# The blocked inverse in the second mixer: its dense chunks gathered in front of it and at its end

## The chip, the cores and the metric

One core of one Trainium2 chip. The metric is device microseconds (us) of one execution of the whole kernel, the median of the runs shown. Lower is better.

## The reference, cut to what matters

The kernel computes two transformer blocks on x of 256 tokens by 1024 features, all in float32. The change lies in the second block's mixer. Its left half (8 heads of 64) is a generalised delta rule, computed in 4 chunks of 64 tokens; its right half (another 8 heads) is softmax attention with forgetting:

```python
p = h @ w_in[l]
p_rwkv = token_shift(p[..., :SHIFT_COLS], shift_mu[l])
p_fox = p[..., SHIFT_COLS:SHIFT_COLS + FOX_COLS]
gates = jax.nn.sigmoid(p[..., SHIFT_COLS + FOX_COLS:])
...
sa = jnp.einsum('bhvk,bhk->bhv', state, a_t)
state = (state * w_t[:, :, None, :]
         + sa[..., :, None] * b_t[:, :, None, :]
         + v_t[..., :, None] * k_t[:, :, None, :])
y_t = jnp.einsum('bhvk,bhk->bhv', state, r_t)
```

Inside a chunk the kernel does not step token by token. It writes the 64 dependent steps as a unit triangular system and inverts that matrix for each of 32 head-chunks: blocks of 2 are inverted first, and 5 levels then double the block size (2 to 64) by X <- X + X N X, where N is the part of the matrix below the blocks (m_b under a mask of `levels`).

## The kernel before, in words

**Weights.** The weights come as chunks of 1 MB (128 x 2048 float32), numbered in the order of their use, in a ring of 3 slots. SyncE loads chunk n once the low part of chunk n-3 is made. ScalarE copies it to `w_hi` (L1489, it waits for the slot's chunk n-3 to be used), VectorE takes the rest, `w_lo = w_raw - w_hi` (L1813), and TensorE runs three matmuls for each product of a step: high by high, high by low, low by high (L2253 to L2255, called `three`). A chunk by `columns` or by tokens is 8 steps (`NT`) of 6 matmuls; these are called dense here. `columns(n, steps=(a, b))` does steps a to b-1 of chunk n, so a chunk can be spread over other work. A dense chunk goes to one of the PSUM banks 0 to 2 (n % 3), and its reader's count `bank.._read` lets the chunk 3 later start.

**The inverse** (`pe_mixer`, L594 to L655). The 16 unit columns of both head halves are treated in two sets, f = 0 and f = 1, of 8 units by 2 heads. For level n (1 to `LEVELS` = 5) and set f:

- GpSimd makes `half_n`, N under the mask of level n (L1457), a level ahead; it signals `off_ready`.
- `first_product(n, f)` on TensorE: N X into PSUM bank 4 (L599). It waits for `off_ready`, for the copy out of bank 4 before, and for `x_added` of level n-1 of its own set. 32 instructions in the trace.
- ScalarE copies bank 4 to `half_1` (L871), signal `p1_copied`.
- `second_product(n, f)` on TensorE (L599 also): X-transposed by that copy into bank 6 or 5, and the transposed result into bank 7 or 3; 64 instructions, and 32 at level 5, where the first of the two is left out. It waits for `p1_copied` and for the bank's reader, `xt_added`.
- `grow(n, f)` on VectorE adds bank 6 or 5 to `x_inv` (L1098, signal `x_added`) and bank 7 or 3 to `xt_inv` (L1101, signal `xt_added`).

Each engine's order is written out by hand. TensorE's order before: `first_product(n,0)`, `second_product(n-1,1)`, `second_product(n,0)`, `first_product(n,1)`, then a piece of a dense chunk. The chunks cut up for this are B_FOX+3 (`fk`, the attention's keys), B_FOX+4 and B_FOX+5 (its values, by tokens) and step 0 of B_GA, the first chunk of gates. ScalarE's queue holds, between the copies of `half_1`, the high parts of chunks B_FOX+5 (level 1), B_FOX+6 = B_GA (level 2) and B_FOX+7 (level 4), and `v_tokens(0)` ahead of level 4, which takes the values of B_FOX+4 out of PSUM (L862). VectorE's holds the low parts of the same chunks and, at level 1, `out_bank(B_FOX+3)` (L1850).

**Around it.** In front stand the chunk scores (L573), transposes (L487, L589) and one step of B_FOX+3. Behind it stands a loop over 4 chunks (L657 to L703, L668 in the trace) in which small products, copies by ScalarE (L878, L880, L882) and sums by VectorE (L1117, L1119) follow one another; step 1 of B_GA lies in its last turn, step 2 behind it (L705), and then the head sums of y (L708) and the rest of the gates.

Of the kernel before, what the change touches and what calls it, by code (L numbers as in the profile page):

```python
# [11 lines left out]
ACT = mybir.ActivationFunctionType  # L12
# [6 lines left out]
NT = D // P  # L19
# [69 lines left out]
def block_pair(nc, inp, out, scratch, shifted):  # L89

    ctx = ExitStack()
    with ctx:
        S = Signals(nc, ctx)
# [5 lines left out]
        bank = [side_banks[b // 2][:, b % 2, :] for b in range(4)]  # L99
# [376 lines left out]
        def pe_mixer(told, pe, state, by_columns, by_tokens, by_rows, rows_to_tokens, turn_late_half, spread):  # L476
            def columns(n, fresh=None, tokens=False, midway=None, steps=(0, NT)):
                if steps[0] == 0:
                    pe.wait_ge(S[f"bank{bank_of[n]}_read"], reads[n] - 1)
                if tokens:  # L480
                    by_tokens(n, n % RING, bank_of[n], steps=steps)
                else:
                    by_columns(n, n % RING, bank_of[n], fresh=fresh, midway=midway, steps=steps)
# [107 lines left out]
                                   start=True, stop=True)  # L591
            mm.then_inc(S["units_turned"], told.one("units_turned"))

            columns(B_FOX + 3, steps=(1, 4))  # L594

            def product(b, left, right, f):
                for i in range(8):
                    for h in range(2):
                        mm = pe.matmul(head(bank[b], h, slice(i * CHUNK, (i + 1) * CHUNK)), left(f, i, h),  # L599
                                       right(f, i, h), start=True, stop=True)  # L600
                return mm
# [13 lines left out]
            def first_product(n, f):  # L615

                done = 2 * (n - 1) + f
                pe.wait_ge(S["off_ready"], done + 1)
                if done > 0:
                    pe.wait_ge(S["p1_copied"], done)  # L620
                if n > 1:
                    pe.wait_ge(S["x_added"], done - 1)
                product(4, n_of, x_of, f).then_inc(S["p1"], told.one("p1"))

            def second_product(n, f):

                done = 2 * (n - 1) + f
                pe.wait_ge(S["p1_copied"], done + 1)
                if n > 1:
                    pe.wait_ge(S["xt_added"], done - 1)  # L630
                if n < LEVELS:
                    product((6, 5)[f], xt_of, p_of, f)
                product((7, 3)[f], p_of, xt_of, f).then_inc(S["p2"], told.one("p2"))
# [1 line left out]
            pe.wait_ge(S["turned_copied"], 8)  # L635
            pe.wait_ge(S["turned_copied"], 6)
            pe.wait_ge(S["forget_read"], 1)
            for n in range(1, LEVELS + 1):
                first_product(n, 0)
                if n == 1:  # L640
                    columns(B_FOX + 3, steps=(4, 5))
                else:
                    second_product(n - 1, 1)
                if n == LEVELS:
                    columns(B_FOX + 5, tokens=True, steps=(4, 6))
                second_product(n, 0)
                first_product(n, 1)
                if n == 1:
                    columns(B_FOX + 3, steps=(5, NT))
                elif n < LEVELS:  # L650
                    columns(B_FOX + 4 + n // 4, tokens=True, steps=(0, 4) if n != 3 else (4, NT))
                else:
                    columns(B_FOX + 5, tokens=True, steps=(6, NT))
            second_product(LEVELS, 1)
            columns(B_GA, steps=(0, 1))  # L655

            for c in range(NCH):  # L657
                def each(fn):
                    for t in range(HT):
                        for h in range(2):  # L660
                            mm = fn(t, h, c * HT + t)
                    return mm

                def cell(b, t, h):
                    return head(bank[b], h, slice(t * CHUNK, (t + 1) * CHUNK))

                def mul(o, left, right, start, stop):
                    return pe.matmul(o, left, right, start=start, stop=stop, skip_group_check=True)  # L668

                def decayed(k, u, h):  # L670
                    return head(ar, h, u, slice(k * CHUNK, (k + 1) * CHUNK))

                pe.wait_ge(S["xt_added"], 2 * LEVELS)
                if c > 0:
                    pe.wait_ge(S["w_copied"], c)
                mm = each(lambda t, h, u: mul(cell(4, t, h), head(m_k, h, u, slice(0, CHUNK)), head(v_tok, h, u),
                                              t == 0, not c and t == HT - 1))
                if c:
                    pe.wait_ge(S["state"], c)
                    mm = each(lambda t, h, u: mul(cell(4, t, h), decayed(0, u, h), head(state_t, h, t), False,  # L680
                                                  t == HT - 1))
                mm.then_inc(S["w_summed"], told.one("w_summed"))
                if c > 0:
                    pe.wait_ge(S["y_copied"], c)
                each(lambda t, h, u: mul(cell(7, t, h), head(v_tok, h, u), head(m_k, h, u, slice(CHUNK, P)),
                                         t == 0, False))
                if c:
                    each(lambda t, h, u: mul(cell(7, t, h), head(state_t, h, t), decayed(1, u, h), False, False))
                pe.wait_ge(S["w_copied"], c + 1)
                if c > 0:  # L690
                    pe.wait_ge(S["sa_copied"], c)
                each(lambda t, h, u: mul(cell(5, t, h), head(xt_inv, h, u), head(w_s, h, t), True, True)).then_inc(
                    S["sa_summed"], told.one("sa_summed"))
                if c < NCH - 1:
                    each(lambda t, h, u: mul(cell(6, t, h), head(k_tok, h, u), head(v_tok, h, u), t == 0, False))
                    pe.wait_ge(S["sa_copied"], c + 1)
                    each(lambda t, h, u: mul(cell(6, t, h), head(b_tok, h, u), head(sa_s, h, t), False,
                                             t == HT - 1)).then_inc(S["state_summed"], told.one("state_summed"))
                if c == NCH - 1:
                    columns(B_GA, steps=(1, 2))  # L700
                pe.wait_ge(S["sa_copied"], c + 1)
                each(lambda t, h, u: mul(cell(7, t, h), head(sa_s, h, t), head(m_b, h, u, slice(CHUNK, P)),
                                         False, t == HT - 1)).then_inc(S["y_summed"], told.one("y_summed"))  # L703

            columns(B_GA, steps=(2, 3))  # L705
            pe.wait_ge(S["y_copied"], NCH)
            for t in range(HT):
                mm = pe.matmul(bank[4 + t // 2][:, t % 2 * T:t % 2 * T + T], head_ones[:, :], y_t[:, t, :],  # L708
# [89 lines left out]
        def act_mixer(told, act, a, split, spread, state):  # L798
# [59 lines left out]
            def v_tokens(j):  # L858

                m = B_FOX + 4 + j  # L860
                act.wait_ge(S["chunk_used"], m + 1)
                v = [a.activation(fv[:, t, 256 * j:256 * j + 256], bank[bank_of[m]][:, t * T:t * T + T],  # L862
                                  ACT.Copy, scale=rcol[:, t:t + 1]) for t in range(TT)]
                v[1].then_inc(S[f"bank{bank_of[m]}_read"], 1)

            for n in range(1, LEVELS + 1):
                if n == 4:
                    v_tokens(0)
                for f in range(2):
                    act.wait_ge(S["p1"], 2 * (n - 1) + f + 1)  # L870
                    a.activation(half_1[:, f, :], bank[4][:, :], ACT.Copy).then_inc(  # L871
                        S["p1_copied"], told.one("p1_copied"))
                if n in (1, 2, 4):
                    split(B_FOX + (5, 6, 6, 7)[n - 1])
            v_tokens(1)
            for c in range(NCH):
                act.wait_ge(S["w_summed"], c + 1)
# [66 lines left out]
        def dve_mixer(told, dve, v, split, diagonals, out_bank, state):  # L944
# [148 lines left out]
            def grow(n, f):  # L1093

                dve.wait_ge(S["p2"], 2 * (n - 1) + f + 1)
                if n < LEVELS:
                    o = flat(x_inv[:, 8 * f:8 * f + 8, :])
                    v.tensor_tensor(o, o, bank[(6, 5)[f]][:, :], ALU.add).then_inc(  # L1098
                        S["x_added"], told.one("x_added"))
                o = flat(xt_inv[:, 8 * f:8 * f + 8, :])  # L1100
                v.tensor_tensor(o, o, bank[(7, 3)[f]][:, :], ALU.add).then_inc(  # L1101
                    S["xt_added"], told.one("xt_added"))

            dve.wait_ge(S["turned_copied"], 8)
            for n in range(1, LEVELS + 1):
                grow(n, 0)
                if n in (1, 2, 4):
                    split(B_FOX + (5, 6, 6, 7)[n - 1])
                if n == 1:
                    out_bank(B_FOX + 3, fk[:, 2:4, :])  # L1110
                grow(n, 1)
            dve.wait_ge(S["xt_added"], told.value("xt_added"))
            for c in range(NCH - 1):
                dve.wait_ge(S["state_summed"], c + 1)
# [1535 lines left out]
```

## Time and profile before

| what | us |
|---|---|
| median of 3 runs | 1122.13 |
| lowest, highest | 1122.07, 1122.37 |
| profiled execution | 1122.54 |
| its span, first to last instruction | 1120.7 |
| outside the span | 1.84 |
| the inverse with its dense pieces, 753.78 to 800.05 | 46.27 |
| the loop over 4 chunks, 800.05 to 814.39 | 14.34 |

Times in the trace count from the span's start. PE is TensorE's matmuls, PEld its weight loads, DVE is VectorE, ACT ScalarE, POOL GpSimd, SP SyncE. Matmuls are pipelined: the durations of neighbours overlap, so the time that a matmul costs is the distance from its start to the next one's start and not its duration. PEclk is the granted clock of TensorE as a share of 2.4 GHz.

### The profile page before, as it was taken

How to read it: one execution, taken by the hardware profiler on the slowest of the kernel's cores; microseconds unless marked ns; L12 is line 12 of the kernel's file. 1: busy time of each engine (PE TensorE's matmuls, PEld its weight loads, DVE VectorE, ACT ScalarE, POOL GpSimd, SP SyncE). 2: the span in 40 equal slices, each digit the busy share in tenths (PEclk: the TensorE clock that was granted, in tenths of full speed). 3: DMA queues.
4: the chain of work that ended last, by engine and by line, in shares of the span. 5: the costliest groups of instructions: out<-in, count | busy, mean ns of one | idle time of the engine just before them, and what ended most of it. 6: DMA issues, size and time to landing. Idle time of an engine off the chain costs nothing.

```text
span 1120.7 us, 20963 instructions
## 1 busy us (share of the span) xinstructions
PE 1108.9 (99%) x8970; PEld 1023.2 (91%) x8970; DVE 770.9 (69%) x1033; ACT 581.5 (52%) x711; POOL 277.3 (25%) x167
## 2 busy tenths in 40 slices
PE   9999999999999999999999999999999999999997
PEld 9999999999999999888888889999999989888886
DVE  4888978757787767776456467984368675564565
ACT  6433344594765545575445448623244656454454
POOL 3888784000000000003313330113030002233132
PEclk9999999999999999999999999999999999999999
DMA  8586553355456555545565564423134444655651
GB/s 271 192 278 212 188 188 113 113 185 185 145 194 207 187 187 187 187 130 190 194 200 183 191 193 153 145 78 115 40 116 149 149 155 152 220 178 194 211 172 52
DMA packets 147150, 190.00 MB, mean 170 GB/s; under 512 B 7659, under 2 KB 132139, under 8 KB 146943
## 3 DMA queue, kind: packets, MB, share of 16 engines
q1 hardware_dynamic: 145743, 184.32, 50.2%
q0 software_dynamic: 1264, 4.55, 1.2%
q8 instruction: 57, 0.93, 0.4%
q14 instruction: 22, 0.18, 0.1%
q10 hardware_dynamic: 64, 0.02, 0.0%
HBM read 187.79 MB, written 2.65 MB: 170 GB/s over the span
## 4 chain that ended last, share of the span: by engine, by line
PE 94%; DVE 3%; ACT 2%; issue 1%; ACTq 0%; DVEq 0%
PE banks L2253 14%; PE banks L2254 14%; PE banks L2255 14%; PE banks L2305 13%; PE banks L2310 7%; PE bank L2420 6%; PE bank L2421 6%; PE bank L2422 6%; PE bank L599 2%; PE bank L668 1%; DVE w_lo L1813 1%; PE bank L2528 1%; PE bank L2255 1%; PE bank L2254 1%; PE bank L2253 1%; PE banks L2421 1%
## 5 line engine op out<-in xcount | busy, mean ns | idle before, releaser
L1489 ACT ACTIVATE w_hi<-w_raw 128x2048 fp32r<-128x2048 f32 x170 | 324.1, 1909 | 84.7 <-PE banks L2255 60.9
L1813 DVE TENSOR_TENSOR w_lo<-w_raw,w_hi 128x2048 fp32r<-128x2048 f32 x144 | 334.7, 2328 | 42.1 <-ACT w_hi L1489 41.7
L2253 PE MATMUL banks<-X_both,w_hi 128*128 128x256 f32 x1120 | 321.3, 287 | 0.6 <-DVE w_lo L1813 0.5
L2254 PE MATMUL banks<-X_both,w_hi 128*128 128x256 f32 x1120 | 316.8, 283 | 0.0
L2255 PE MATMUL banks<-X_both,w_lo 128*128 128x256 f32 x1120 | 316.8, 283 | 0.0
L2253 PEld LDWEIGHTS banks<-X_both,w_hi 128*128 128x128 f32 x1120 | 214.5, 192 | 5.1 <-issue 2.6
L2254 PEld LDWEIGHTS banks<-X_both,w_hi 128*128 128x128 f32 x1120 | 214.6, 192 | 0.5
L2255 PEld LDWEIGHTS banks<-X_both,w_lo 128*128 128x128 f32 x1120 | 214.5, 192 | 0.0
L2305 PE MATMUL banks<-X_both,w_hi 128*128 128x512 f32 x640 | 201.0, 395 | 0.2 <-DVE w_lo L1813 0.2
L1426 POOL TENSOR_TENSOR arena<-arena,rstd 128x512 f32<-128x512 f32 x20 | 65.4, 3270 | 502.7 <-DVE arena L1946 502.7
L2310 PEld LDWEIGHTS banks<-X_both,w_lo 128*128 128x128 f32 x640 | 120.2, 188 | 28.2
L2310 PE MATMUL banks<-X_both,w_lo 128*128 128x256 f32 x640 | 125.7, 278 | 0.0
L1946 DVE TENSOR_TENSOR arena<-banks,arena 128x512 f32<-128x512 f32 x40 | 27.6, 691 | 134.4 <-ACT arena L1633 134.4
L1383 POOL TENSOR_TENSOR w_lo<-w_raw,w_hi 128x2048 fp32r<-128x2048 f32 x23 | 106.7, 4647 | 33.7 <-ACT w_hi L1489 33.6
L2420 PE MATMUL bank<-w_hi,Y_hi 128*128 128x512 f32 x264 | 103.2, 391 | 1.2 <-DVE Y_lo L1978 1.2
L2421 PE MATMUL bank<-w_hi,Y_lo 128*128 128x512 f32 x264 | 102.9, 390 | 0.0
L2422 PE MATMUL bank<-w_lo,Y_hi 128*128 128x512 f32 x264 | 102.7, 389 | 0.0
L2305 PEld LDWEIGHTS banks<-X_both,w_hi 128*128 128x128 f32 x640 | 98.8, 189 | 2.0 <-issue 0.6
L2055 DVE SCALAR_TENSOR_TENSOR bank<-arena,par,bank 128x256 f32<-128x256 f32 x232 | 93.2, 483 | 0.6
L1599 ACT ACTIVATE arena<-arena,par 128x256 f32<-128x256 f32 x44 | 24.1, 595 | 69.5 <-DVE arena L1942 69.5
L1633 ACT ACTIVATE arena<-banks 128x512 f32<-128x512 f32 x40 | 24.0, 599 | 69.1 <-PE banks L2310 69.1
L2420 PEld LDWEIGHTS bank<-w_hi,Y_hi 128*128 128x128 f32 x264 | 49.6, 188 | 11.0 <-DVE Y_lo L1978 1.6
(334 smaller groups left out, 1627.5 us busy)
## 6 DMA issues: line engine op xcount, KB each, us to landing
w_raw<-in_ffn_w_dram SPq DMA_DIRECT2D x66, 1024.0 KB, 5.2
w_raw<-in_w_in_dram SPq DMA_DIRECT2D x52, 1024.0 KB, 5.1
w_raw<-in_w_up_dram SPq DMA_DIRECT2D x22, 1024.0 KB, 5.1
w_raw<-in_w_down_dram SPq DMA_DIRECT2D x11, 1024.0 KB, 5.0
w_raw<-in_w_out_dram SPq DMA_DIRECT2D x8, 1024.0 KB, 4.9
w_raw<-in_conv_pw_w_dram SPq DMA_DIRECT2D x4, 1024.0 KB, 4.9
w_raw<-in_w_attn_out_dram SPq DMA_DIRECT2D x2, 1024.0 KB, 5.0
w_raw<-in_rwkv_proj_dram SPq DMA_DIRECT2D x2, 1024.0 KB, 4.8
```

What stands on the lines that cost most here:

```text
L1383: g.tensor_tensor(w_lo[n % RING][:, :], raw[n % RING][:, :], w_hi[n % RING][:, :].bitcast(F32), ALU.subtract).then_inc(S["w_lo_pool"], tol ...
L1489: a.activation(w_hi[slot][:, :], raw[slot][:, :], ACT.Copy).then_inc(S["w_hi"], told.one("w_hi"))
L1813: v.tensor_tensor(w_lo[slot][:, :], raw[slot][:, :], w_hi[slot][:, :].bitcast(F32), ALU.subtract).then_inc(S["w_lo"], told.one("w_lo"))
L2055: v.scalar_tensor_tensor(out=conv[:, t, :] if k == CONV_W - 1 else part, in0=src, scalar=w, in1=part, op0=ALU.mult, op1=ALU.add).then_inc( ...
L2253: pe.matmul(o, wh, xh, start=start, stop=False, skip_group_check=True)
L2254: pe.matmul(o, wh, xl, start=False, stop=False, skip_group_check=True)
L2255: return pe.matmul(o, wl, xh, start=False, stop=stop, skip_group_check=True)
L2305: pe.matmul(side_banks[1 - side][:, m, :].rearrange("p (a t) -> p a t", a=2), w_hi[slot][:, c:c + P], X_both[:, :, k, :], start=k == 0, st ...
L2310: mm = pe.matmul(side_banks[1 - side][:, m, T:2 * T], w_lo[slot][:, c:c + P], X_hi[:, k, :], start=False, stop=k == NT - 1, skip_group_che ...
L2420: pe.matmul(o, yh, wh, start=first and k == 0, stop=False, skip_group_check=True)
L2421: pe.matmul(o, yl, wh, start=False, stop=False, skip_group_check=True)
L2422: mm = pe.matmul(o, yh, wl, start=False, stop=last, skip_group_check=True)
```

## The change

TensorE's order becomes: all of B_FOX+3; `first_product(1,0)`, `first_product(1,1)`, `second_product(1,0)`; then for levels 2 to 5 `first_product(n,0)`, `second_product(n-1,1)`, `second_product(n,0)`, `first_product(n,1)` with nothing dense between; all of B_FOX+4; `second_product(5,1)`; all of B_FOX+5. The steps of B_GA move back by one: step 0 into the loop's last turn, steps 1 and 2 behind it. `first_product(n,1)` gets a bank of its own, the one that B_FOX+5 will use, in place of bank 4. ScalarE and VectorE keep the same instructions in another order: the parts of B_FOX+5 after level 1, of B_FOX+6 inside level 2, of B_FOX+7 after level 5, and ScalarE's `v_tokens(0)` after level 5.

```diff
-            columns(B_FOX + 3, steps=(1, 4))
+            columns(B_FOX + 3, steps=(1, NT))
...
                 pe.wait_ge(S["off_ready"], done + 1)
-                if done > 0:
-                    pe.wait_ge(S["p1_copied"], done)
                 if n > 1:
+                    pe.wait_ge(S["p1_copied"], done - 1)
                     pe.wait_ge(S["x_added"], done - 1)
-                product(4, n_of, x_of, f).then_inc(S["p1"], told.one("p1"))
+                elif f == 1:
+                    pe.wait_ge(S[f"bank{bank_of[B_FOX + 5]}_read"], reads[B_FOX + 5] - 1)
+                product((4, bank_of[B_FOX + 5])[f], n_of, x_of, f).then_inc(S["p1"], told.one("p1"))
...
-            for n in range(1, LEVELS + 1):
+            first_product(1, 0)
+            first_product(1, 1)
+            second_product(1, 0)
+            for n in range(2, LEVELS + 1):
                 first_product(n, 0)
-                if n == 1:
-                    columns(B_FOX + 3, steps=(4, 5))
-                else:
-                    second_product(n - 1, 1)
-                if n == LEVELS:
-                    columns(B_FOX + 5, tokens=True, steps=(4, 6))
+                second_product(n - 1, 1)
                 second_product(n, 0)
                 first_product(n, 1)
-                if n == 1:
-                    columns(B_FOX + 3, steps=(5, NT))
-                elif n < LEVELS:
-                    columns(B_FOX + 4 + n // 4, tokens=True, steps=(0, 4) if n != 3 else (4, NT))
-                else:
-                    columns(B_FOX + 5, tokens=True, steps=(6, NT))
+            columns(B_FOX + 4, tokens=True)
             second_product(LEVELS, 1)
-            columns(B_GA, steps=(0, 1))
+            columns(B_FOX + 5, tokens=True)
...
                 if c == NCH - 1:
-                    columns(B_GA, steps=(1, 2))
+                    columns(B_GA, steps=(0, 1))
...
-            columns(B_GA, steps=(2, 3))
+            columns(B_GA, steps=(1, 3))
...
             for n in range(1, LEVELS + 1):
-                if n == 4:
-                    v_tokens(0)
                 for f in range(2):
                     act.wait_ge(S["p1"], 2 * (n - 1) + f + 1)
-                    a.activation(half_1[:, f, :], bank[4][:, :], ACT.Copy).then_inc(
+                    a.activation(half_1[:, f, :], bank[(4, bank_of[B_FOX + 5])[f]][:, :], ACT.Copy).then_inc(
                         S["p1_copied"], told.one("p1_copied"))
-                if n in (1, 2, 4):
-                    split(B_FOX + (5, 6, 6, 7)[n - 1])
+                    if (n, f) in ((1, 1), (2, 0)):
+                        split(B_FOX + 4 + n)
+            v_tokens(0)
+            split(B_FOX + 7)
             v_tokens(1)
...
                 grow(n, 0)
-                if n in (1, 2, 4):
-                    split(B_FOX + (5, 6, 6, 7)[n - 1])
+                if n in (1, 2):
+                    split(B_FOX + 4 + n)
                 if n == 1:
                     out_bank(B_FOX + 3, fk[:, 2:4, :])
                 grow(n, 1)
+            split(B_FOX + 7)
```

## Rows read from the trace of the kernel before

**Rows 1.** The page's first part: busy time, share of the span, instructions.
```profile
span 1120.7 us, 20963 instructions
PE 1108.9 (99%) x8970; PEld 1023.2 (91%) x8970; DVE 770.9 (69%) x1033; ACT 581.5 (52%) x711; POOL 277.3 (25%) x167
```

**Rows 2.** The chain that ended last: shares of the span by engine.
```profile
PE 94%; DVE 3%; ACT 2%; issue 1%; ACTq 0%; DVEq 0%
```

**Rows 3.** Busy time by stretch: PE, PEld, DVE, ACT, POOL, clock, DMA share, GB/s.
```profile
735.00:751.77 16.77, 16.77 (x354) 16.44 (x352) 13.73 (x20) 2.96 (x6) 0.02 (x1) 1.00 0.15 44
...
772.22:781.03 8.81, 8.81 (x217) 8.61 (x216) 4.35 (x5) 1.20 (x2) 2.96 (x2) 1.00 0.39 123
...
753.78:800.05 46.27, 46.27 (x1045) 44.53 (x1041) 20.53 (x23) 14.16 (x19) 14.40 (x9) 1.00 0.30 93
800.05:814.39 14.34, 14.03 (x433) 13.14 (x433) 2.12 (x5) 3.84 (x10) 0.00 (x0) 1.00 0.02 5
```

**Rows 4.** PE's groups by form, from 753.78 to 800.05.
```profile
L599 PE MATMUL bank<-arena 64*64 64x64 f32 x736 | 23.5, 219 | 0.0
L2253 PE MATMUL banks<-w_hi,X_both 128*128 128x256 f32 x32 | 9.6, 299 | 0.0
...
L599 PE MATMUL banks<-arena 64*64 64x64 f32 x160 | 5.5, 219 | 0.0
L2253 PE MATMUL banks<-X_both,w_hi 128*128 128x256 f32 x16 | 4.9, 308 | 0.0
```

**Rows 5.** The chain in order of time: the transposes of L487.
```profile
745.33 5.60 PE bank L487 x192
```

**Rows 6.** PE in order of time: start, us, line, operation (levels 1 and 2).
```profile
756.13 1.15 PE L599 MATMUL bank<-arena 64*64 64x64 f32 x32
...
758.12 3.02 PE L599 MATMUL bank<-arena 64*64 64x64 f32 x96
...
775.07 2.97 PE L599 MATMUL bank<-arena 64*64 64x64 f32 x96
777.97 0.39 PE L2253 MATMUL banks<-w_hi,X_both 128*128 128x256 f32 x1
778.19 0.28 PE L2254 MATMUL banks<-w_lo,X_both 128*128 128x256 f32 x1
778.31 0.28 PE L2255 MATMUL banks<-w_hi,X_both 128*128 128x256 f32 x1
```

**Rows 7.** ACT in order of time, with the idle time before.
```profile
757.32 0.60 ACT L871 ACTIVATE arena<-bank 128x512 f32<-128x512 f32 x1 [2.34 <-PE bank L599]
...
798.17 0.84 ACT L862 ACTIVATE arena<-banks,rcol 128x256 f32<-128x256 f32 x2 [1.02 <-PE banks L2255]
800.78 0.38 ACT L878 ACTIVATE arena<-bank 128x256 f32<-128x256 f32 x1 [1.77 <-PE bank L668]
```

**Rows 8.** DVE in order of time.
```profile
752.43 2.75 DVE L1813 TENSOR_TENSOR w_lo<-w_raw,w_hi 128x2048 fp32r<-128x2048 f32 x1
760.31 0.69 DVE L1098 TENSOR_TENSOR arena<-arena,bank 128x512 f32<-128x512 f32 x1 [5.14 <-PE bank L599]
...
763.61 2.29 DVE L1813 TENSOR_TENSOR w_lo<-w_raw,w_hi 128x2048 fp32r<-128x2048 f32 x1 [2.01 <-ACT w_hi L1489]
...
777.15 0.69 DVE L1098 TENSOR_TENSOR arena<-arena,bank 128x512 f32<-128x512 f32 x1 [0.58 <-PE bank L599]
...
807.60 0.42 DVE L1119 TENSOR_TENSOR arena<-arena,small 128x256 f32<-128x256 f32 x1
...
821.92 4.28 DVE L1813 TENSOR_TENSOR w_lo<-w_raw,w_hi 128x2048 fp32r<-128x2048 f32 x1 [0.81 <-ACT w_hi L1489]
```

**Rows 9.** POOL in order of time: the mask of a later level.
```profile
757.37 1.30 POOL L1457 TENSOR_TENSOR arena<-arena,levels 128x512 f32<-128x512 f32 x1 [1.04 <-PE bank L599]
```

**Rows 10.** PE's weight loads in the loop over chunks, with the idle before.
```profile
801.21 1.01 PEld L668 LDWEIGHTS bank<-arena 64*64 64x64 f32 x32 [0.15 <-ACT arena L878]
...
808.08 1.01 PEld L668 LDWEIGHTS bank<-arena 64*64 64x64 f32 x32 [0.26 <-DVE arena L1119]
```

## The prediction, made before the changed kernel was run

> **What bounds the kernel now.** I read the busy shares first, then the chain, then the stretch around the change. TensorE is busy for 1108.9 of 1120.7 us [rows 1] and carries 94% of the chain that ended last [rows 2]; a change counts by what it does to TensorE's own order. In the changed stretch, 753.78 to 800.05, PE is busy for all of its 46.27 us at clock 1.00 [rows 3], so there is no idle time to win back. What is there to win shows only in start distances. A dense matmul costs 0.12 us (778.19 to 778.31 [rows 6]). A small instruction costs 5.60 / 192 = 0.0292 us where 192 stand in a row [rows 5]. One level, 772.22 to 781.03, is 8.81 us [rows 3] for 192 small instructions (5.61) and 24 dense ones (2.88): 0.32 is left over. Over the whole stretch there are 736 + 160 = 896 small instructions and 3 x (32 + 16) = 144 dense ones, the three lines of `three` having the same count [rows 4], 26.16 + 17.28 = 43.44 us, and 2.83 are left. The stretch holds 9 dense pieces, counted in the code: 0.314 each. It is the cost of going from small to dense and back; the first dense matmul of a piece alone takes 0.22 instead of 0.12 (777.97 to 778.19 [rows 6]).
>
> **What is removed.** Of the 9 pieces 3 remain: B_FOX+3, B_FOX+4, B_FOX+5. Step 0 of B_GA goes to the loop's last turn, and steps 1 and 2 stand together behind it, where before one step stood in each place, so nothing is added there. 6 x 0.314 = **1.88 us** saved. All instructions stay. One dense step (0.72 us) leaves the stretch and comes back behind the loop, at nothing: PE was issuing there without a gap before too, and every chain of the other engines that starts after the loop's y sums starts from PE's order as before.
>
> **What is added: waits that dense work covered.** A first product is 32 x 0.0292 = 0.94 us, a second 1.88. A copy by ScalarE starts 1.19 after its first product starts (756.13, 757.32), takes 0.60 [rows 6, 7] and is seen by PE 0.05 later (800.78 + 0.38, 801.21 [rows 7, 10]): 1.84. VectorE starts 2.19 after a second product starts that follows dense work (758.12, 760.31), 2.08 after one that follows small work (775.07, 777.15), takes 0.69 for x [rows 6, 8] and is seen 0.06 later (807.60 + 0.42, 808.08 [rows 8, 10]): 2.83 to 2.94, I take 2.85.
>
> - `second_product(1,0)` waits for its copy, 1.84, behind two first products, 1.88: nothing.
> - `first_product(2,0)` stands straight behind `second_product(1,0)` and needs its sum: 2.85 - 1.88 = **0.97** idle. No work covers this one. Getting under way again is in the 0.06.
> - `first_product(n,0)` for n = 3, 4, 5 has `first_product(n-1,1)` in front: 2.85 - 1.88 - 0.94 = 0.03 each. `second_product(n-1,1)`, n = 3, 4, 5, needs a copy at 1.84 with 1.88 in front (its own first product and the next): 0. `first_product(n,1)` and `second_product(n,0)` have 1.88 in front of what they need beyond their partner: nothing. I take **0.1** in all, for waits that end within 0.05 us of their cover.
> - VectorE's queue at levels 1 and 2. Call S the start of `first_product(1,0)`. ScalarE copies set 1 until S+2.7 and makes the high part of B_FOX+5 until S+4.6. VectorE sums set 0 until S+5.3, makes the low part (2.29 alone, 2.75 with GpSimd beside it [rows 8]) until 7.6 to 8.0, `out_bank` until 8.2 to 8.7, and has x of set 1 at 8.9 to 9.3. `first_product(2,1)` wants it at S + 4.85 + 0.94 + 1.88 + 1.88 = 9.55: covered. The sum of level 2, set 0, may then start 0.2 late and hold `first_product(3,0)`: **0.1**. The low part of B_FOX+6 comes after that sum, from 11.2 to 13.5, just when set 1 of level 2 is ready, and PE wants that sum at about 15.2: covered. ScalarE's two high parts delay no copy by this timetable.
> - GpSimd's mask for the next level takes 1.30 after a first product [rows 9], and PE wants it after at least 2.9: nothing; at later levels it has 5 us.
> - `v_tokens(1)`, 0.84 [rows 7], now starts some 0.1 after the loop's first instruction and ends at 0.95; the loop's first copy stands behind it, and it started at 0.73 before (800.78 [rows 7] in a loop that began at 800.05 [rows 3]): **0.2** later, which nothing covers. The chunk parts of B_FOX+7, 1.9 and 2.3 us, go after level 5 and lie beside B_FOX+5, 5.8 us; the load that waits for them is issued some 5 us later than before and is not wanted until about 30 us on.
>
> Sum: -1.88 + 0.97 + 0.1 + 0.1 + 0.2 = -0.51, **-0.5 us**. The profiled execution's span would be 1120.2 of 1120.7. That execution took 1122.54, 0.41 above the median, so I subtract from the median: 1122.13 - 0.5 = **1121.6**.
>
> **Bounds.** The waits that stand bare in this kernel are those of the loop over chunks: 14.34 us less 433 small instructions (12.64) [rows 3] leaves 1.7 us over some 11 waits, 0.16 each. If each of the 8 tight places (n = 2 to 5, both kinds) cost that, the waits are 1.3 instead of 0.1 and the sum +0.7. If the tight ones cost nothing and the 0.97 stays, it is -0.9. Forecast's own range: 1121.2 to 1122.8.
>
> **Rivals.** (1) **VectorE's low parts are late.** Both stand between sums that PE now wants within a level, with no dense piece beside. If they take 4.28 us, as one does at 821.92 with GpSimd busy beside it [rows 8], x of set 1 comes at S+10.95 instead of 9.0 (PE waits 1.4), the next sum of set 0 costs 0.3 more, and behind the second low part `first_product(3,1)` waits 0.95: +2.65, in all +2.1, **1124.3**. It decides from a low part of about 2.9 us on. For it: GpSimd's masks of level 3 run just then. Against: with such a mask beside it the low part took 2.75, and 4.28 goes with GpSimd's larger additions. (2) **The clock falls.** From S to the end of `first_product(5,1)` TensorE would run some 27 us of small products and short waits, without the dense pieces that break them up now. Against: the loop over chunks is 14.34 us of nearly only these, with waits, at 1.00, and 735.00 to 751.77, with 12.7 us of them, too [rows 3]. If the clock went to its lower level, 1.2 GHz, for the 12 us beyond the longest stretch shown, these would cost between nothing and double, 0 to 12 us; I take the middle, **1127.6**. The Trainium skill, "TensorE: Matmul & The Clock Gate", section "A second HAM failure mode: psum-queue depth-cycling", reports a kernel whose frequent micro-idles between groups of matmuls made its clock swing between its two levels; by that rule the short waits added here speak against the change. The loop's rows are the nearest case, and they speak against the rule at this size. (3) **The cover is better than I reckon**: the one bare wait is filled or half as long and the changeovers are worth all of 1.88: **1120.6** at best. No faster outcome has a mechanism here: all that can be saved is 1.88.
>
> **How the numbers follow.** A measurement of this kernel can tell about 0.2% from no change, 2.2 us. Forecast 0.70, rival 1 0.12, rival 2 0.04, rival 3 0.09, and 0.05 for a cause outside the stretch, of either sign. Faster by over 2.2 us is out of reach of the savings: 0.04. Slower by over 2.2 takes rival 2, half or more of rival 1 and some of the rest: 0.12. Within: 0.84. The range takes in the forecast's own and rival 3 and part of rival 1: 1120.4 to 1123.4.
>
> **What would show it.** Right: L599's 896 instructions run from about 759.1 with PE idle once for about 1 us, ended by VectorE's L1098; later levels about 5.65 to 5.8 us each instead of 8.81; the loop starts near 798.7; clock 1.00. Wrong: levels of 6 us or more (waits at every level), a low part (L1813) over 2.9 us between 763 and 773, a clock under 1.00, or a later stage that takes another time than before.

## The result, and the profile after

The changed kernel takes 1126.49 us in the median (1125.89 to 1127.05, 6 runs) against 1122.10 of the kernel before (1121.62 to 1122.43, 6 runs, 3 of them beside it): the ratio is 1.0039, 95% interval 1.0028 to 1.0050. It is 4.4 us slower. The forecast was 1121.6 us and no measurable change, with a range that ended at 1123.4.

The busy time of every engine is the same as before [rows 1]; the span is 4.5 us longer.

```profile
span 1125.2 us, 20963 instructions
PE 1108.4 (99%) x8970; PEld 1023.2 (91%) x8970; DVE 770.9 (69%) x1033; ACT 581.4 (52%) x711; POOL 279.0 (25%) x167
```

The changed stretch by windows, in the same columns as [rows 3]: the dense chunk in front, the small products, the two dense chunks at the end with the last product between them, the three together, and the loop over chunks.

```profile
753.60:758.82 5.22, 5.22 (x45) 5.09 (x42) 1.38 (x1) 1.09 (x2) 2.54 (x1) 1.00 0.53 169
758.82:790.77 31.95, 27.09 (x866) 26.23 (x865) 16.80 (x20) 8.98 (x11) 13.44 (x8) 1.00 0.24 74
790.77:803.74 12.97, 12.97 (x132) 12.64 (x129) 2.98 (x2) 3.24 (x4) 0.00 (x0) 1.00 0.06 14
753.60:803.74 50.14, 45.28 (x1038) 43.96 (x1035) 21.16 (x23) 13.31 (x17) 15.97 (x9) 1.00 0.22 69
803.74:818.19 14.45, 14.03 (x434) 13.14 (x433) 2.12 (x5) 4.57 (x12) 0.00 (x0) 1.00 0.20 66
```

The stretch has grown from 46.27 to 50.14 us, +3.87. The loop takes 14.45 instead of 14.34, +0.11. What lies behind it, from its end to the end of the span, takes 307.01 instead of 306.31, +0.70: the dense step that the change moved there. It began 0.18 earlier. Together that is the whole 4.5. TensorE, never idle in this stretch before, is now busy for 27.09 of the 31.95 us of small products, at clock 1.00 throughout.

What ended those idle times, in the list of waits from 750 to 830 (who waited for whom: total, times, longest):

```profile
PEld bank L599 <- issue: 3.5, 3, 2.0
PE bank L599 <- issue: 2.3, 2, 2.0
PEld banks L599 <- issue: 1.8, 1, 1.8
PE banks L599 <- issue: 1.6, 1, 1.6
PE bank L599 <- DVE arena L1092: 1.0, 1, 1.0
```

The wait for VectorE's sum is the one that the forecast named. The others end in "issue": TensorE waited for nothing that another engine had to deliver. Its matmuls in order of time (L599; start, duration, count, idle time before) show where:

```profile
763.72 2.08 PE L599 MATMUL bank<-arena 64*64 64x64 f32 x64 [0.95 <-DVE arena L1092]
...
771.36 0.28 PE L599 MATMUL banks<-arena 64*64 64x64 f32 x3
773.28 1.08 PE L599 MATMUL banks<-arena 64*64 64x64 f32 x29 [1.64 <-issue]
774.15 2.08 PE L599 MATMUL bank<-arena 64*64 64x64 f32 x64
776.01 1.15 PE L599 MATMUL banks<-arena 64*64 64x64 f32 x32
777.10 0.24 PE L599 MATMUL bank<-arena 64*64 64x64 f32 x1
779.29 2.02 PE L599 MATMUL bank<-arena 64*64 64x64 f32 x62 [1.95 <-issue]
...
783.54 1.09 PE L599 MATMUL bank<-arena 64*64 64x64 f32 x31 [0.30 <-issue]
```

None of the three stands at the border of a product: the group at 771.36 ends after 3 matmuls of a product of 32, the one at 777.10 after 1 of 64, where no wait is written. Between them lie 29 + 64 + 32 + 1 = 126 matmuls, between the second and the third 127, by the lines that the excerpt leaves out. That spacing points to the instructions themselves. The list of DMA queues has one called `q8 instruction`, whose packets are 16 KB each. In the 31.95 us of small products 7 of them move while TensorE runs 866 + 865 matmuls and weight loads, 247 for a packet; in the 46.27 us of the kernel before it is 8 packets and 2086 instructions [rows 3], 261 for a packet. So I read q8 as the queue that brings TensorE's program, one packet for some 127 small matmuls with a weight load each. The DMA lines from 766 to 771.5 (busy tenths in 40 slices, then the queues):

```profile
DMA  0000000000296956999999999999999997710000
...
q1 hardware_dynamic: 1040, 1.05, 59.6%
q8 instruction: 1, 0.02, 1.2%
```

A weight load of 1 MB fills the DMA engines from 767.5 to 770.8, and the one instruction packet moves only as it ends. The trace has a start and an end for each packet of q8, and they fit all three stops:

| the packet moves | a weight load beside it | TensorE goes on | after the packet's end |
|---|---|---|---|
| 770.72 to 771.79 | 767.4 to 771.0 | 773.28 | 1.49 us |
| 776.78 to 777.88 | 774.1 to 777.5 | 779.29 | 1.41 us |
| 780.93 to 782.12 | none | 783.54 | 1.42 us |

The two long stops, 3.59 us, follow packets that moved only as a weight load ended. The third, 0.30 us, has no load beside it.

### The profile page after: what moved, and what is told of

Read it like the earlier page. It is cut to its first block, busy times and chain, and to the rows that moved or that the text cites. A ratio compares the mean times of both kernels' runs of the same rounds, so it can differ in the third digit from the quotient of the medians.

```text
span 1125.2 us, 20963 instructions
## 1 busy us (share of the span) xinstructions
PE 1108.4 (99%) x8970; PEld 1023.2 (91%) x8970; DVE 770.9 (69%) x1033; ACT 581.4 (52%) x711; POOL 279.0 (25%) x167
## 4 chain that ended last, share of the span: by engine, by line
PE 94%; DVE 3%; ACT 2%; issue 1%; ACTq 0%; DVEq 0%
PE banks L2248 14%; PE banks L2249 13%; PE banks L2250 13%; PE banks L2300 13%; PE banks L2305 7%; PE bank L2415 6%; PE bank L2416 6%; PE bank L2417 6%; PE bank L599 2%; PE bank L662 1%; DVE w_lo L1808 1%; PE banks L599 1%; PE bank L2523 1%; PE bank L2250 1%; PE bank L2249 1%
## 5 line engine op out<-in xcount | busy, mean ns | idle before, releaser
L2250 PE MATMUL banks<-X_both,w_lo 128*128 128x256 f32 x1120 | 316.8, 283 | 0.0
L2250 PEld LDWEIGHTS banks<-X_both,w_lo 128*128 128x128 f32 x1120 | 214.5, 192 | 0.0
```

The lines of the kernel that those rows point to most:

```text
L2250: return pe.matmul(o, wl, xh, start=False, stop=stop, skip_group_check=True)
```

## The experiments

The theories were these. **Theory 1**: an instruction packet must be there every 127 small matmuls, 3.7 us; it comes late when it meets a weight load, and the dense pieces of the kernel before, where 127 matmuls took 5 us and more, hid that. **Theory 2**: the supply is too slow for small products whatever else moves. **Theory 3**: misnamed waits on VectorE or ScalarE. Each experiment was timed beside the kernel before, whose median was 1121.87 for e1 to e4, 1122.10 for e5 to e8 and 1122.19 for e9 and e10.

**e1: the weight loads held.** In the diffs `...` marks what is left out.

```diff
...
 sp.wait_ge(S["w_lo"], n - (BY_POOL + 2))
+if n == B_FOX + 8:
+    sp.wait_ge(S["p1"], 2 * LEVELS)
```

> The changed kernel, but SyncE holds the loads of chunks B_FOX+8 and later until all ten first products are done (some 16 us later than now; they are wanted 30 us later still). Theory 1: TensorE's own instructions arrive in transfers of 16 KB, one for about 127 small matmuls with their weight loads, and the two idle times of 1.64 and 1.95 us at 771.6 and 777.3 that the trace ends by 'issue' are transfers queued behind a 1 MB weight load: both vanish, 1126.5 - 3.4 = 1123.1 us. Theory 2: the supply is too slow for small products by itself, whatever else moves: idle times and 1126.5 us stay. Theory 3: they are waits for VectorE or ScalarE that the trace misnames: 1126.5 us stay.

Measured: 1122.33 us (1121.34 to 1123.24, 10 runs), ratio 1.0003 (0.9993 to 1.0013). Against the changed kernel that is -4.2 us, or -3.9 when each is taken against the kernel before that ran beside it (4.39 and 0.46 above it). The small products by windows (as above), and the DMA lines of 9 us in their midst:

```profile
758.16:785.80 27.64, 26.62 (x865) 26.04 (x865) 16.71 (x20) 8.98 (x11) 13.46 (x8) 1.00 0.03 9
752.93:798.76 45.83, 44.81 (x1038) 43.76 (x1034) 21.08 (x23) 13.31 (x17) 16.01 (x9) 1.00 0.24 76
```

```profile
DMA  0000000300000000000000030000000000000000
...
q8 instruction: 2, 0.03, 1.6%
```

With the order of the change untouched the small products take 27.64 us instead of 31.95. Both long stops are gone. In these 9 us two instruction packets move and nothing else. Theories 2 and 3 expected no change and fall as explanations of the 4 us. Something is left to theory 2: one level in this kernel, 774.57 to 780.83, took 6.26 us where its neighbour took 5.74. In it the weight loads pause once:

```profile
778.82 0.95 PEld L599 LDWEIGHTS bank<-arena 64*64 64x64 f32 x30 [0.17 <-issue]
```

The packet in front of that moved from 776.26 to 777.47, with nothing else in the queues, and 1.35 us later the weight loads went on. So a packet can be late by itself, but then it costs 0.5 us here, and 0.30 in the changed kernel's third stop, and not 1.6 to 1.9.

**e2: one more transfer of 1 MB in the changed kernel.**

```diff
...
+if n == B_FOX + 9:
+    sp.wait_ge(S["p1"], 6)
+    sp.dma_start(spare.rearrange("(k p) c -> p k c", p=P),
+                 inp["w_out_2"][0, :, 0:256].rearrange("(k p) c -> p k c", p=P)).then_inc(
+        S["spare_moved"], 16)
...
```

> The changed kernel with one more 1 MB transfer that nobody reads (DRAM to DRAM, from SyncE's queue), released by the sixth first product, at about 777, so that it runs to about 782 or later, over the next instruction transfer, near 781, where now nothing else moves. Theory 1 (instruction transfers queue behind weight loads): one more idle time by 'issue' of 1 to 3 us between 780 and 790, 1127.5 to 1129.5 us. Theories 2 (supply rate alone) and 3 (misnamed waits): no new idle time, 1126.5 us.

Measured: 1126.81 us (1124.48 to 1127.44, 4 runs), ratio 1.0044 (1.0027 to 1.0061). The profiled run was the lowest of the four, 1124.48. Its chain:

```profile
770.96 1.08 issue
780.08 1.12 issue
```

A stop at 780 is new, with a packet that moved at 778.78, while the two transfers filled the queues from 773.4 to 781.9. But the stop of 1.95 us at 777 is gone, as its packet moved at 773.42, just as they began. The expectation is met for the profile's new stop and not for the time. The runs spread over 3 us, so this run decides nothing; it shows that the cost depends on which packet meets which load.

**e3: B_FOX+4 behind level 3.**

```diff
                 first_product(n, 1)
-            columns(B_FOX + 4, tokens=True)
+                if n == 3:
+                    columns(B_FOX + 4, tokens=True)
             second_product(LEVELS, 1)
```

> The changed kernel with the whole of B_FOX+4 moved from behind level 5 to behind level 3, loads as they are. Same instructions, same number of changeovers. Theories 1 and 2: the dense chunk stands near 777 and gives the supply 5.8 us for 48 matmuls, so the idle time of 1.95 us at 777.3 and the smaller one of 0.30 go, the 1.64 at 771.6 stays: 1126.5 - 2 = 1124.5 us. Theory 3 (waits of the product chains): levels 4 and 5 keep theirs, about 1126.5 us less what the chunk covers at one place, at most 0.5.

Measured: 1125.64 us (1124.56 to 1126.65, 6 runs), ratio 1.0033 (1.0020 to 1.0045): -0.85 instead of -2. The waits of TensorE:

```profile
PE banks L599 <- issue: 1.3, 1, 1.3
PE banks L599 <- ACT arena L864: 0.7, 1, 0.7
PE banks L2250 <- issue: 0.7, 1, 0.7
```

The first stop, which was to stay at 1.64, is 1.34 here. The stop of 1.95 has become 0.7 and has moved into the dense chunk (L2250): dense work at that place does help. But `second_product(5,1)` now stands straight behind `first_product(5,1)`, and waits 0.7 us for ScalarE's copy; the move took its cover away. My expectation had left that out.

**e4: a dense piece at the one bare wait.**

```diff
-            columns(B_FOX + 3, steps=(1, NT))
+            columns(B_FOX + 3, steps=(1, 5))
...
             second_product(1, 0)
+            columns(B_FOX + 3, steps=(5, NT))
             for n in range(2, LEVELS + 1):
```

> The changed kernel with steps 5 to 7 of B_FOX+3 moved behind second_product(1,0), where TensorE waits 0.95 us for VectorE's sum. All theories: that wait goes, one changeover of 0.31 comes back, -0.64 us. Theory 3 expects no more: 1125.9 us. Theories 1 and 2: the 18 dense matmuls use the running instruction transfer up 1.6 us more slowly, so the idle time at 771.6 may shrink as well: 1124.3 to 1125.9 us.

Measured: 1122.10 us (1121.60 to 1122.63, 10 runs), ratio 1.0002 (0.9992 to 1.0011): -4.4 us, twice the largest gain expected. The wait for VectorE is gone (-0.95 + 0.31 for the changeover), and of 3.89 us of stops by "issue" one of 0.30 is left, though the weight loads run as in the changed kernel:

```profile
778.32 1.09 PE L599 MATMUL bank<-arena 64*64 64x64 f32 x31 [0.30 <-issue]
```

2.2 us of dense work early in the stretch shift when a packet is wanted against when it moves. A packet still moves as the first load ends, from 767.50 to 768.58, but TensorE comes to that border only at 769.74, 1.2 us later; in the changed kernel it had stopped there at 771.64, and the packet ended at 771.79. The next one, at 771.35, moved before the second load, which began at 772.5. The third moved as that load ended, from 775.78 to 776.89, and has the stop of 0.30 behind it.

**e5: loads held, 2 MB moved over the small products.** The edit is that of e1 and, after the load of B_FOX+7, a transfer as in e2 with columns 0 to 511, released by `p1` at 3.

> The kernel of e1 (changed order, weight loads held: 1122.33 us) with 2 MB that nobody reads moved DRAM to DRAM from SyncE's queue, released by the third first product, near 764, so that the DMA queues are full from about 766 to 776, across two or three instruction transfers. Theory 1 (instruction transfers wait behind bulk transfers): idle times by 'issue' of 1 to 2 us each come back at two or three places, 1124.5 to 1127 us. Theory 1b (it was not the queue but what the held weights do otherwise: SBUF writes, slots, semaphores): nothing comes back, 1122.3 us.

Measured: 1125.80 us (1125.38 to 1126.52, 7 runs), ratio 1.0034 (1.0022 to 1.0045): +3.5 over e1. PE in order of time, and the DMA lines from 764 to 778:

```profile
770.79 0.28 PE L599 MATMUL banks<-arena 64*64 64x64 f32 x3
773.50 1.39 PE L599 MATMUL banks<-arena 64*64 64x64 f32 x29 [2.43 <-issue]
```

```profile
DMA  1000099699999999999998410000000100000000
...
q8 instruction: 3, 0.05, 1.4%
...
spare<-in_w_out_dram SPq DMA_DIRECT2D x1, 2048.0 KB, 9.5
```

One stop of 2.43 us comes back, after the same third instruction as in the changed kernel; its packet ended at 772.15, 1.35 us before TensorE went on. The transfer touches no SBUF, no slot and no semaphore that a compute engine waits for, so theory 1b falls. There was one stop instead of two or three. The rest of the time lies behind it and has another cause, in the same columns as [rows 3]:

```profile
773.50:774.59 1.09, 1.09 (x30) 1.09 (x31) 0.00 (x0) 0.00 (x0) 0.09 (x1) 0.77 0.00 0
774.59:777.78 3.19, 3.19 (x69) 3.19 (x68) 1.28 (x2) 0.00 (x0) 0.00 (x0) 0.54 0.02 5
777.78:780.75 2.97, 2.97 (x103) 2.92 (x101) 1.28 (x2) 1.19 (x2) 1.74 (x2) 1.00 0.02 6
```

The granted clock fell to its lower level, 1.2 GHz, from 774.09 to 777.51. Just before, TensorE had stood idle for the 2.43 us and then run 0.6 us of small products. The product of 64 that starts at 774.59 takes 3.19 us instead of 1.87 (e6, 771.64 to 773.51), the 29 matmuls in front of it 1.09 instead of 0.87: 1.5 us by the clock. With the stop that is 3.9, less the 0.5 us of e1's slow level, which is not slow here: 3.4 of the 3.5 us. It is not only the profiled run: over a whole execution 6 of the 7 runs of e5 had a mean granted clock of 0.996 or 0.997, and all others in this document 0.998 or 0.999, but for one run of the changed kernel and one of e2 (0.997 each).

**e6: e1 and e4 together.**

> The kernel of e1 with the dense piece of e4 (steps 5 to 7 of B_FOX+3 behind second_product(1,0)). If both effects are separate and the rest of the arrangement is worth what the prediction reckoned: -0.64 for the wait against the changeover, and a few tenths less idle by 'issue': 1121.3 to 1121.7 us, just under the kernel before (1121.9). If e4 had already all that the supply can give (its own rest was 0.30 us): the same as e4, 1122.1 us.

Measured: 1121.24 us (1120.59 to 1121.64, 10 runs), ratio 0.9992 (0.9982 to 1.0001). The stretch and two levels without a dense piece:

```profile
753.77:798.27 44.50, 44.50 (x1038) 43.57 (x1034) 21.07 (x23) 13.30 (x17) 14.68 (x9) 1.00 0.25 78
768.82:774.58 5.76, 5.76 (x195) 5.71 (x193) 5.60 (x6) 1.19 (x2) 4.55 (x2) 1.00 0.01 3
774.58:780.33 5.75, 5.75 (x195) 5.70 (x193) 2.56 (x5) 1.20 (x2) 2.50 (x2) 1.00 0.02 6
```

TensorE is never idle in it. 44.50 plus the moved step of 0.72 is 45.22 against 46.27 before. This is the arrangement at the value that the forecast reckoned with.

**e7 and e8: the two controls on the kernel before**, with the hold of e1 alone, and with the 2 MB of e5 as well.

> Control: the kernel before with the loads of B_FOX+8 and later held until all ten first products are done, as in e1. Theory 1: its dense pieces give every instruction transfer time enough, so nothing waits for one and nothing is gained: 1121.9 us, within 0.5. If holding the loads helped for a reason that has nothing to do with the order, it gains some 4 us here too.

> Control: the kernel of e7 with the 2 MB of e5, released by the third first product. Theory 1: an instruction transfer that comes up to 3 us late is still in time in the dense-and-small order, where 128 matmuls last 5 us: 1121.9 to 1123 us, at most one short idle time by 'issue'. If bulk transfers slow small products directly, as much as in e5: 1124 us or more.

Measured: e7 1123.43 us (1122.95 to 1124.58, 10 runs), ratio 1.0014 (1.0004 to 1.0023); e8 1123.25 us (1123.04 to 1123.88, 10 runs), ratio 1.0011 (1.0002 to 1.0021). The 2 MB cost nothing (-0.2) where the small products are broken up by dense pieces, and 3.5 us in e5 where they are not. So a bulk transfer does not slow small products as such. The hold did not gain either, but it cost 1.3 us, which was not expected. The chain of e7 in the loop over chunks says why:

```profile
801.53 2.72 PE bank L668 x85
804.25 1.11 issue
805.36 1.49 PE bank L668 x43
```

In this order the tenth first product comes late, so the held loads ran beside the loop, whose products are small too, and a packet was late there. Before, no load ran beside it. e8 has the same stop, 0.85 us at 804.72. The cause was moved into another place and made its cost there.

**e9 and e10: a version that is faster than both.** e9 is e6 with step 0 of B_GA in front of the loop again; e10 is the same without the hold.

```diff
             columns(B_FOX + 5, tokens=True)
+            columns(B_GA, steps=(0, 1))
...
-                    columns(B_GA, steps=(0, 1))
+                    columns(B_GA, steps=(1, 2))
...
-            columns(B_GA, steps=(1, 3))
+            columns(B_GA, steps=(2, 3))
```

> The kernel of e6 (1121.24 us) with step 0 of B_GA back in front of the loop over chunks, steps 1 and 2 where the kernel before had them. No changeover is added. ScalarE's v_tokens(1) (0.84 us) then runs beside dense work and the loop's first copy starts after 0.73 us instead of 0.9 to 1.0: -0.1 to -0.3 us, 1121.0 us.

> The same without the hold on the loads (e4 with the step of B_GA in front of the loop). Separates what the hold is worth once a dense piece stands early: e4 had 1122.1 us and one idle time by 'issue' of 0.30. If instruction transfers that meet a weight load are still late in a few places: 1121.8 us, 0.5 to 0.9 above e9. If the hold is worth nothing there: the same as e9.

Measured: e9 1121.16 us (1120.59 to 1121.52, 11 runs), ratio 0.9991 (0.9982 to 1.0000); e10 1122.21 us (1121.60 to 1122.61, 11 runs), ratio 1.0000 (0.9991 to 1.0009). e9 is the lowest of all, 1.0 us under the kernel before and 5.3 under the changed one, but the interval touches 1. What the step itself brings, -0.08 against e6, can't be told from nothing. The hold is worth 1.05 us here; e10's chain has a stop of 0.52 at 770.63. Matmul by matmul, e10's trace falls behind e9's in this stretch at three places, by 0.72, 0.31 and 0.13 us, and they are the instructions at which the changed kernel stopped: the same three borders of packets.

## Why the prediction was wrong, step by step

- **"What is added: waits that dense work covered"** is the step that failed. It counted every semaphore that TensorE waits for and took 0.0292 us for each small instruction as granted for 27 us on end. What the dense pieces had covered was also the arrival of TensorE's own program. The rows that gave the price, 192 instructions in a row [rows 5], cover one and a half packets with slower work in front. The term left out measured 3.89 us of stops, and holding the loads gave back 4.2 us (e1). That the dense pieces covered it is shown by the pair e5 and e8: the same 2 MB cost 3.5 us without them and nothing with them.
- Of the semaphore waits the sizes were right. `first_product(2,0)`: 0.97 forecast, 0.95 measured. The levels were to take 5.65 to 5.8 us; 5.75 and 5.76 in e6, where nothing was late. VectorE's low parts held up nobody in the changed kernel: the one of B_FOX+6 took 3.20 us at 769.85, over the 2.9 from which rival 1 was to decide, and no wait for VectorE followed. The stops are not the reason: in e1 and e6, which have none there, the same part took 3.20 and 3.19 us, and TensorE waited for VectorE no more than before. In e1 the sum behind it ended at 772.99, 14.8 us after the start of `first_product(1,0)` (758.16), and the forecast had PE want it at about 15.2. So 2.9 was too low a bar for this part.
- **Changeovers and the whole arrangement**: with the supply mended and the bare wait filled (e6), the stretch takes 44.50 us. The forecast's terms give 43.44 - 0.72 + 4 x 0.314 + 0.1 + 0.1 = 44.18. The terms of the sum were good to 0.3 us, and the sign would have been right.
- `v_tokens(1)` was to cost 0.2; the first copy of the loop starts 0.83 after the loop's first instruction (804.57 - 803.74) instead of 0.73, so 0.1, which is also what the loop grew by.
- **Bounds.** The price of a wait in the loop, 0.16 us, was taken for the upper end of every unknown. It is a price for semaphores and holds nothing about the queue that feeds the program. The packets were visible in the kernel before, 8 in its 46.27 us; I had not asked how many TensorE would need in the new order: 7 in 31.95 us.
- **Rival 2** did not come about in the changed kernel: 1.00 in each of its windows above, through 27 us of small products with idle times of up to 1.95 us between them. Its outcome, clearly slower, came from another mechanism. But it was no empty rival: in e5, behind one stop of 2.43 us, the clock did fall, for 3.4 us, and cost 1.5. Rival 1 had the nearest time, 1124.3, for a wrong reason.
- The rule that stood beside rival 2, from the Trainium skill, "TensorE: Matmul & The Clock Gate", section "A second HAM failure mode: psum-queue depth-cycling", is not borne out by the changed kernel: three idle times of 0.95 to 1.95 us and one of 0.30 at clock 1.00. e5 has a fall to the lower level behind an idle time, but one fall behind one stop and no swinging.

The Trainium skill, "Runtime: NRT & Kernel Launch", section "Instruction fetch mechanics", says that programs are refilled in 16 KiB blocks of 256 instructions and that crossing a block's border is mostly hidden, since the sequencer issues more slowly than blocks arrive. The block's size agrees with the trace: 57 packets, 0.93 MB in q8 (none is recorded from 354 to 477 and from 540 to 664 us, so the whole program had more), and some 250 instructions for a packet in the stretches above. That the crossing is hidden holds for the kernel before in this stretch, where TensorE is never idle, and fails for the small products of the changed one: three stops, 3.89 us.

## What to carry to other kernels

Before work that issues small instructions back to back is made denser, count its instructions against the instruction packets (here one for 127 small matmuls, 3.7 us of them) and look at what bulk transfers run beside it: a dense piece may be covering the supply of the program and not only the copies that it was put there for. An idle time that ends in "issue", in the midst of a product where no wait is written, was that supply in every case here. To check it, compare its end with the end of the last instruction packet. Holding weight loads until the small run is over gave back 4.2 us with one wait, but only where they then did not meet the next small run (e7).

## What the runs showed of the hardware that was not expected

- TensorE goes on 1.3 to 1.6 us after the end of a late instruction packet: 1.33 to 1.56 in all twelve stops of this kind, in the changed kernel and in the profiles of e2, e3, e4, e5, e7, e8 and e10.
- The instruction supply runs only about one packet ahead. Between 771.8 and 774.1 the DMA queues of the changed kernel were empty, and yet the packet that TensorE wanted at 777.3 had not moved:

```profile
DMA  0000000000000000000000000000000000000000
...
DMA packets 0, 0.00 MB, mean 0 GB/s; under 512 B 0, under 2 KB 0, under 8 KB 0
```

- Without bulk transfers beside it the supply just keeps up with 64 x 64 matmuls: no idle time in e6, but 0.5 us in one level of e1.
- Bulk transfers delay these packets whoever they belong to: SyncE's loads to SBUF (1.64 and 1.95 us of stops) and a copy from DRAM to DRAM (2.43). The packet starts late and is not slower once it moves: 1.07 and 1.10 us for the two that followed loads, 1.19 for the one without. Whether it waits behind the load's descriptors on its own DMA engine was not tried.
- The granted clock of TensorE stayed at 1.00 through stops of 1.64 and 1.95 us and fell to 0.50 for 3.4 us behind the stop of 2.43 (e5). Whether the stop brought the fall about was not tried by itself.
- Where a packet and a load meet by chance, one profile does not stand for the median: the four runs of e2 spread over 3.0 us, and the profiled one was the lowest.
